# Start of the mixers in a two-model kernel on one core: spread rows on 128 partitions, GpSimd's part moved to ScalarE and VectorE, a new order of the query products

## The reference, cut to what matters

```python
gc = jnp.cumsum(g.reshape(b, h, n, chunk), axis=-1)
diff = gc[..., :, None] - gc[..., None, :]
decay = jnp.where(incl, jnp.exp(jnp.where(incl, diff, 0.0)), 0.0)
a_mat = jnp.where(strict, jnp.einsum("bhncd,bhnsd->bhncs", k, k) * decay * beta[..., :, None], 0.0)
rhs = jnp.concatenate([v * beta[..., None], k * (beta * jnp.exp(gc))[..., None]], axis=-1)
sol = lax.linalg.triangular_solve(a_mat + jnp.eye(chunk, dtype=a_mat.dtype), rhs,
                                  left_side=True, lower=True, unit_diagonal=True)
qk = jnp.einsum("bhncd,bhnsd->bhncs", q, k) * decay
```

## Time and profile before

| | us |
|---|---|
| median of 3 runs | 942.94 |
| lowest and highest of them | 936.97 and 943.37 |
| the profiled execution | 941.03 |
| its span, first to last instruction | 939.5 |
| PE busy in it | 920.4 |

### The profile page before, as it was taken

One profiled execution on the slowest core, in us unless ns is written; L12 is line 12 of the kernel. 1 busy time (PEld: TensorE's weight loads), 2 busy tenths in 40 slices (PEclk: granted clock), 3 DMA queues, 4 the chain that ended last, 5 costly groups with the idle time before them and its releaser, 6 DMA issues.

```text
span 939.5 us, 16653 instructions
## 1 busy us (share of the span) xinstructions
PE 920.4 (98%) x6746; PEld 816.9 (87%) x6746; DVE 630.4 (67%) x959; ACT 479.4 (51%) x839; POOL 104.4 (11%) x114
## 2 busy tenths in 40 slices
PE   8999999999999999999999999999999999999997
PEld 8988778877998999998888789989778899999885
DVE  5974376546895678778864477987665666666643
ACT  6334447446654565556743566654544555444432
POOL 1000032001320000101410004311000011111001
PEclk9999999999999999999999999998999999999999
DMA  8745445554555784432025453522110455555551
GB/s 323 279 158 180 138 158 173 175 179 167 182 209 189 269 288 161 148 123 90 1 91 182 176 179 136 180 90 89 49 47 13 167 202 187 209 189 184 202 197 45
DMA packets 23520, 150.41 MB, mean 160 GB/s; under 512 B 3564, under 2 KB 3848, under 8 KB 6168
## 3 DMA queue, kind: packets, MB, share of 16 engines
q1 hardware_dynamic: 23104, 149.20, 45.7%
q10 hardware_dynamic: 344, 0.18, 0.1%
HBM read 148.30 MB, written 1.05 MB: 159 GB/s over the span
## 4 chain that ended last, share of the span: by engine, by line
PE 83%; DVE 9%; ACT 4%; issue 2%; DMA 1%; POOL 0%; SPq 0%; ACTq 0%; POOLq 0%; DVEq 0%
PE psum L793 79%; DVE ring_parts L2130 3%; PE psum L874 1%; ACT R L1873 1%; DVE R L2460 1%; ACT high_parts L1684 1%; PE psum L1223 1%; DMA h<-in_x 1%; DVE R L2412 1%; ACT Pf L2050 0%; DVE PTb_parts L2431 0%; DVE R L2470 0%; PE psum L1567 0%; DVE PTb L2624 0%; ACT tmp L1722 0%
## 5 line engine op out<-in xcount | busy, mean ns | idle before, releaser
L2130 DVE TENSOR_TENSOR ring_parts<-ring,high_parts 128x1024 fp32r<-128x1024 f32 (+1 forms) x272 | 331.3, 1257 | 150.0 <-ACT high_parts L1684 148.7
L1684 ACT CAST high_parts<-ring 128x1024 fp32r<-128x1024 f32 x268 | 268.4, 1051 | 182.6 <-PE psum L793 146.1
L793 PE MATMUL psum<-xT_parts,high_parts 128*128 128x256 f32 (+1 forms) x1024 | 230.2, 286 | 2.8 <-DVE nw L2544 2.0
L793 PE MATMUL psum<-xT_parts,ring_parts 128*128 128x256 f32 (+1 forms) x704 | 198.6, 282 | 0.0
L793 PEld LDWEIGHTS psum<-xT_parts,high_parts 128*128 128x128 f32 x1024 | 174.5, 191 | 5.1 <-DVE ring_parts L2130 3.0
L793 PE MATMUL psum<-high_parts,R_parts 128*128 128x512 f32 (+1 forms) x528 | 165.0, 386 | 0.0
L793 PE MATMUL psum<-R_parts,high_parts 128*128 128x256 f32 x832 | 156.0, 277 | 0.0
L793 PE MATMUL psum<-high_parts,xT_parts 128*128 128x512 f32 x480 | 154.2, 397 | 0.0
L793 PEld LDWEIGHTS psum<-xT_parts,ring_parts 128*128 128x128 f32 x704 | 134.0, 190 | 0.1
L793 PEld LDWEIGHTS psum<-R_parts,high_parts 128*128 128x128 f32 x832 | 130.2, 188 | 0.0
L793 PEld LDWEIGHTS psum<-high_parts,R_parts 128*128 128x128 f32 (+1 forms) x528 | 98.8, 188 | 20.5
(11 more groups left out here) (363 smaller groups left out, 1055.7 us busy)
## 6 DMA issues: line engine op xcount, KB each, us to landing
ring<-in_weights SPq DMA_DIRECT2D x135, 1024.0 KB, 4.9
h<-in_x SPq DMA_DIRECT2D x4, 256.0 KB, 4.7
ring<-in_weights SPq DMA_DIRECT2D x4, 256.0 KB, 6.4
ring<-in_weights SPq DMA_DIRECT2D x2, 512.0 KB, 7.7
G<-in_gains SPq DMA_DIRECT2D x2, 512.0 KB, 7.6
out<-xn SPq DMA_DIRECT2D x2, 512.0 KB, 2.6
R<-in_ret_tabs SPq DMA_DIRECT2D x1, 768.0 KB, 13.5
G<-in_p_t SPq DMA_DIRECT2D x1, 512.0 KB, 6.7
```

Source lines behind the costliest of these rows:

```text
L793: return pe.matmul(out, lhsT, rhs, start=first, stop=last, skip_group_check=True)
L1684: act.copy(as_r(hi), value).then_inc(sem("units_high"), 1)
L2130: return dve.tensor_tensor(as_r(value), value, value_of(hi), ALU.subtract)
```

## The change

1. Spread rows: the row and the column of the identity are taken on all 128 partitions; the other 124 of the row are zero. POOL fills the two places with zeros once, much earlier, and ACT and DVE wait for that before they write the rows (`row_zeros`).
2. POOL's part goes: X and Y are started by ACT in the item `tok`, and the first level's mask is multiplied by DVE in the item `A`.
3. In `("Lz", 0, c)` DVE subtracts from Y first and from X after it; PE waits for the three X (`first_x`) before the second level's `Lx`.
4. The order: `fv 1` goes ahead of `Q 1`, `fv 2` ahead of `Qm 1`, and `fv 3` is made in halves of its sum over channels, the first between `Q 2` and `Qm 2`, the second after `kv 1`.

```diff
-    order += [("Q", 1), ("fv", 1), ("Qm", 1), ("Q", 2), ("fv", 2), ("Qm", 2), ("kv", 1), ("fv", 3), ("kv", 2), ("Fs", 0),
-              ("kv", 0)]
+    order += [("fv", 1), ("Q", 1), ("fv", 2), ("Qm", 1), ("Q", 2), ("fvh", 3), ("Qm", 2), ("kv", 1), ("fv", 3), ("kv", 2),
+              ("Fs", 0), ("kv", 0)]
...
+        FILLED = {"NU": R[:, R4 + 1024 + TM:R4 + 1024 + 2 * TM], "UQ": Pf[:, 2 * TM:3 * TM]}
...
             def spread_rows(bank, rows, src, c):
                 t0, n = CHUNKS[c]
                 for hd in range(GH):
-                    mm(bank[0:rows, hd * n:(hd + 1) * n], ident[0:4, hd:hd + 1].to_broadcast([4, rows]),
-                       SM[src][:, t0:t0 + n], hd == 0, False)
+                    ins = mm(bank[0:rows, hd * n:(hd + 1) * n], ident[:, hd:hd + 1].to_broadcast([P, rows]),
+                             FILLED[src][:, t0:t0 + n], hd == 0, False)
+                return ins
...
-                for hd in range(GH):
-                    ins = mm(bank[:, hd * n:(hd + 1) * n], ident[0:4, hd:hd + 1].to_broadcast([4, P]),
-                             SM["UQ"][:, t0:t0 + n], hd == 0, False)
-                ins.then_inc(sem("query_rows"), 1)
+                spread_rows(bank, P, "UQ", c).then_inc(sem("query_rows"), 1)
...
-            def channels_input(name, j):
+            def channels_input(name, j, k0=0, k1=KD):
...
-                bank = main.open(pe, (name, j))
+                bank = main.at((name, j)) if k0 else main.open(pe, (name, j))
...
-                for k in range(KD):
+                for k in range(k0, k1):
...
-                main.full(ins, (name, j))
+                if k1 == KD:
+                    main.full(ins, (name, j))
...
+                    if lv == 1:
+                        pe.wait_ge(sem("first_x"), 3)
...
             def soft_exponentials():
                 act.wait_ge(sem("gates_biased"), 1)
+                act.wait_ge(sem("row_zeros"), 1)
...
                 elif kind == "tok":
+                    for c, (_, n) in enumerate(CHUNKS):
+                        for base in (0, C_ALL):
+                            c0 = base + C_OFF[c]
+                            act.copy(PTb[0:n, c0:c0 + 4 * n].rearrange("p (h n) -> p h n", h=GH),
+                                     over(ident[0:n, 0:n], GH)).then_inc(sem("xy_init"), 1)
                     act.wait_ge(sem("columns"), 1)
...
                 wait_read(dve, aux, ("ss", 1))
+                dve.wait_ge(sem("row_zeros"), 2)
...
+                    wait_read(dve, aux, ("kk", c))
+                    dve.tensor_tensor(four(level_rows(0, c)), four(PTb[0:n, a0:a0 + 4 * n]),
+                                      over(tab[0:n, TB_LEVEL:TB_LEVEL + n], GH), ALU.mult).then_inc(sem("level_part"), 1)
...
                     bank = aux.wait(dve, ("z", 0, c))
+                    dve.wait_ge(sem("xy_init"), 6)
                     X = PTb[0:n, C_OFF[c]:C_OFF[c] + 4 * n]
-                    dve.tensor_tensor(X, X, level_rows(0, c), ALU.subtract)
                     for Y, z in corrected(0, c, bank):
                         ins = dve.tensor_tensor(Y, Y, z, ALU.subtract)
                     aux.free(ins, ("z", 0, c))
+                    dve.tensor_tensor(X, X, level_rows(0, c), ALU.subtract).then_inc(sem("first_x"), 1)
...
                 if jj == 4:
+                    pool.memset(FILLED["NU"], 0.0).then_inc(sem("row_zeros"), 1)
+                    pool.memset(FILLED["UQ"], 0.0).then_inc(sem("row_zeros"), 1)
                     pool.memset(nw[:, :], 0.0).then_inc(sem("query_zeros"), 1)
...
-            aux.wait(pool, ("ss", 1))
-            for c, (t0, n) in enumerate(CHUNKS):
-                for base in (0, C_ALL):
-                    c0 = base + C_OFF[c]
-                    pool.tensor_copy(PTb[0:n, c0:c0 + 4 * n].rearrange("p (h n) -> p h n", h=GH),
-                                     over(ident[0:n, 0:n], GH)).then_inc(sem("xy_init"), 1)
-            for c in level_chunks(0):
-                n = CHUNKS[c][1]
-                wait_read(pool, aux, ("kk", c))
-                a0 = 2 * C_ALL + C_OFF[c]
-                pool.tensor_tensor(level_rows(0, c).rearrange("p (h n) -> p h n", h=GH),
-                                   PTb[0:n, a0:a0 + 4 * n].rearrange("p (h n) -> p h n", h=GH),
-                                   over(tab[0:n, TB_LEVEL:TB_LEVEL + n], GH), ALU.mult).then_inc(sem("level_part"), 1)
```

More of the change, by code:

```diff
@@ L1510, in _ @@
             for kind, *key in mixer_order():
-                if kind in ("fin", "fv"):
-                    channels_input(kind, *key)
+                if kind == "fvh":
+                    channels_input("fv", *key, 0, 4)
+                elif kind in ("fin", "fv"):
+                    channels_input(kind, *key, 4 if (kind, key) == ("fv", [3]) else 0)
                 elif kind == "vT":
```

## The result

| | before | changed |
|---|---|---|
| median of 8 runs | 940.57 us | 934.70 us |
| lowest and highest | 936.97 and 943.66 | 932.01 and 937.81 |
| profiled execution | 941.03 | 935.33 |
| mean granted clock in it | 0.992 | 0.996 |

The ratio is 0.9945, with a 95% interval of 0.9928 to 0.9963: 5.2 us (3.5 to 6.8) less, 0.55%. The forecast was 934.6 us. Of 76 executions of the kernel before that were made beside the experiments, one took 3215.5 us, at a clock of 1.000; it stays out of what follows, and the others took 937.25 to 943.77.

The account below looks back on a forecast made before the run. PE, busy for 98% of the span, was taken as the bound. Gains of 1.7 + 1.37 + 1.09 + 3.10 less 0.9 make 6.4 us off the profiled 941.03, so 934.6 us, range 932 to 939.5.

Parts of the forecast that it names:

- The sum: Whole kernel: gains 1.7, 1.37, 1.09 and 3.10 less 0.9 make 6.4 us, from 941.03 to 934.6 us.
- The copies, 1.7 us: PE's 2.0 us wait at `fin 4`: without POOL's copies DVE's slow product shortens, gaining 1.7 us.
- The level parts on DVE: First level: 1.9 us more DVE work, but PE does not wait, with 0.2 us to spare.
- Y ahead of X, and `fv 1` ahead of `Q 1`: At `Q 1`: the wait goes, 1.09 us, and the low clock through `Q 1` and `fv 1`, 3.10 us.
- `fv 3` in halves: Ahead of `kv 0`: PE waits about 0.8 us for DVE, and the second level loses 0.9 us.
- The clock: Low-clock stretches at `A 1`/`fin 7` and `Q 1`/`fv 1` both go, worth 1.37 and 3.10 us.
- 128 rows: Spreads at `A 1`: matmuls cost nothing more, and full rows keep the clock up, gaining 1.37 us.
- A: Rival: rows don't matter to the clock, the fall at `A 1` and `fin 7` stays; 936.0 us, chance 0.16.
- the first fall: Low clock from the key products of chunk 1 into `fin 7`; predicted to go, 1.37 us.
- B: Rival: the clock falls anew around `kv 0`, costing 1.4 to 3.1 us; about 937 us, chance 0.18.
- C: Rival: DVE becomes the bound at the level parts and then `kv 0`; 942.1 us, chance 0.05.
- D: Rival: no loss at `kv 0`, the `fin 4` wait wholly gone, low clock worth 0.5 us more; 932.9 us, chance 0.15.

Follow-up runs that it names:

- only_copies: Kernel before with only the six copies that start X and Y moved from POOL to ACT; median 938.11 us, ratio 0.9979.
- only_level: Kernel before with only the first level's mask products (level parts) on DVE in place of POOL; median 938.98 us, ratio 0.9998.
- old_order: Changed kernel with the item order of the kernel before (`Q 1` ahead of `fv 1`, `fv 3` whole); median 935.85 us, ratio 0.9952 to before.
- only_order: Kernel before with only the new item order and `fv 3` in halves, X still ahead of Y; median 937.88 us, ratio 0.9978.
- rows4: Changed kernel with its spread rows on 4 partitions again; median 935.19 us, ratio 0.9949 to before.
- long4: Changed kernel with 4-row spreads and the spread of `A 2` made six times in place of once; 947.53 and 947.83 us.
- long128: Changed kernel, 128 rows kept, with the spread of `A 2` made six times in place of once; median 938.49 us.
- only_rows: Kernel before with only the spread rows on 128 partitions, zeros by POOL; median 939.34 us, ratio 0.9993.

## Why the prediction was right, point by point

**The sum.** 934.6 us was forecast and 934.7 measured. The agreement is closer than the working deserves, and part of it is luck. The sum was made against an execution of 941.03, 0.9 us above the mean of the 75 runs of before, and the execution profiled afterwards took 935.33. Between these two executions, from the sums over channels to `gz`, 8.41 us were gained up to the mask of `Q 2` (with the half of `fv 3` that is done by then) where 7.26 were forecast, 0.73 were lost behind it where 0.9 were, and 1.32 went to a low stretch that the sum has not. The three errors cancel: 8.41 - 0.73 - 1.32 = 6.36, the very sum of the forecast.

**The copies, 1.7 us.** Right in size and cause. From the sums to `fin 4` it was 615.75 - 608.66 = 7.09 us and is 614.59 - 609.24 = 5.35: 1.74. only_copies shows the cause by itself. What is late next is ACT's cast, as said. ACT's copies took 2.47 us inside the wait.

**The level parts on DVE.** Right, with little to spare: the last is written at 635.93 and PE, through with `fv 0` at 636.17, asks for it at 636.77. only_level shows it without the rest of the change: no wait for a level part there either. That POOL's level parts would themselves have become late, once PE comes sooner, was not in the prediction; only_copies showed it.

**Y ahead of X, and `fv 1` ahead of `Q 1`.** The wait of 1.09 us is gone, with Y of chunk 1 ready at 638.31 and asked for at 640.16. old_order shows that the order did this and Y first did not: without the new order the wait is 1.26.

**`fv 3` in halves.** A loss of 0.9 us was predicted. The mask of `Q 2` came 46.17 us after the sums (654.83 - 608.66) and comes at 39.27, with 1.51 us of `fv 3` done by then that was not before: a gain of 8.41. At the second level it is 7.68, so 0.73 us were lost.

**The clock.** This is where the working was off, though the sum came out. It took the profiled execution's two falls, 1.37 + 3.10 us, as what the kernel before pays there every time and the changed one never. In the profiled executions those two places gained that much and a little more (1.15 + 1.79 + 1.50 for `fin 7`, `Q 1` and `fv 1` alone). But over the runs the change brings 2.9 ± 0.9 us in the low clock's cost by the table's estimate (6.3 before, 3.4 after), and 1.8 ± 0.6 by what 0.001 of clock costs in the runs. Each part alone has less of it than before, by 0.5 to 1.3 us with errors of 0.6 to 0.7, too rough to say what each brings. What made the error good lies beside the clock: 1.7 + 1.09 - 0.9 = 1.9 us were predicted there, and it is 2.5 ± 0.4 by the one and 3.6 ± 0.3 by the other way of reckoning. Spreads that take 1.05 us in place of 1.13 to 1.15 are a part of the rest; the remainder is not traced.

The profiles, one execution of each of the thirteen kernels, show how often a place has a fall. At `A 1` or `fin 7` it is 3 of the 6 kernels with 4-row spreads (before, only_order, rows4) and none of the 7 with 128 rows. Behind the 2.0 us wait at `fin 4` it is 2 of 4, and behind a wait of 0.3 us there none of 9. At `Q 1`, with a wait ahead of it, it is 3 of 5, and with `fv 1` ahead in place of the wait none of 8. Behind the second level's first products it is 2 of 13 (changed and long4), and far behind, in the levels, 5 of 13, with and without the change. only_order has one more near its start, at 9 to 14 us. Rows, copies and order thus each have a place where the fall comes less often with them, though these counts are small.

**128 rows.** The cause was right and its size here was not settled. long4 and long128 show that many matmuls with 4 rows in a row bring the clock down with PE busy, and the counts at `A 1` point the same way. In the kernel itself the rows are worth 0.9 ± 1.0 us (changed against rows4) and 0.7 ± 0.7 us (only_rows against before), and 1.37 had been counted at `A 1` alone with a part of the 3.10 besides.

**The rivals.** A falls with long4, and no profile with 128 rows has the first fall. B, the clock falling around `kv 0`, is what the profiled execution of the changed kernel shows, at 1.32 us, and it lies 0.7 us above the forecast. C did not come: PE waited nowhere for a level part. D's 932.9 is reached by the two runs with a mean clock of 0.999 (932.01 and 932.90), but not by D's mechanism: in the profile the first wait is 0.31 us and 0.73 are lost around `kv 0`, and those two runs have no trace.

## What to carry to other kernels

Where PE is nearly always busy, read its granted clock in stretches before anything else, and find what lies ahead of each fall: here a wait, small tiles, or matmuls with few rows, of which only the last was shown to be enough by itself. A fall that one profile shows is not there in every execution, so its stretch is an upper bound for the gain. Judge by the mean clock over many runs, and take what the clock costs from how these runs scatter, not from (1 - clock) x time. An engine off the critical path (POOL here) can hold up another one by its mere activity: look for operations of one form that take several times their usual length, and for what ran beside them.

## What the runs showed of the hardware that was not expected

- A matmul's rows count for the clock. In one profiled execution each, 48 records with 4 rows, with PE never waiting between them, brought it to half speed and 48 with 128 rows did not. The 4-row piece took 6.32 us and the other 5.52, since the fall came within it (full clock up to 634.50, 0.57 behind that). In the kernel before it fell at `A 1` as well with no wait ahead. The Trainium skill's page "TensorE: Matmul & The Clock Gate", Part 1, gives busy time and idle gaps as what moves the clock and names no rows; by it both kernels would have kept the full clock here, so the measurement decides.
- Whether the clock falls behind a given wait differs between executions of one kernel. The 2.0 us wait at `fin 4` left it at 1.00 in the kernel before and was followed by a low stretch in only_rows and only_order, and in only_level it was not. Over 75 runs of one kernel the mean granted clock lay between 0.990 and 0.998. At the 0.61 us for 0.001 that these runs show, 0.008 makes 4.9 us, most of the distance between its fastest and slowest run (6.5 us).
- Rows of zeros serve the clock: 124 of long128's 128 rows are zero, and its clock held where long4's fell.
